# Every second tile of four residual additions moved from VectorE to GpSimd, in a two-model float32 kernel

## The reference, cut to what matters

```
x = x + _rms_norm(mix, norm_mix_post[layer])
hn = _rms_norm(x, norm_ffn_pre[layer])
x = x + _rms_norm(_squared_relu_mlp(hn, mlp_w1[layer], mlp_w2[layer]), norm_ffn_post[layer])
```

## Time and profile before

| | |
|---|---|
| median of 3 runs | 3810.01 us (3808.03 to 3811.25) |
| profiled execution, its own time | 3813.62 us |
| its span, first to last instruction | 3811.7 us |
| mean granted TensorE clock | 0.980 of full speed |
| busy: TensorE, VectorE, ScalarE, GpSimd | 95%, 49%, 31%, 8% of the span |

### The profile page before, as it was taken

One profiled execution on the slowest core, in us unless ns is written; L12 is line 12 of the kernel. 1 busy time (PEld: TensorE's weight loads), 2 busy tenths in 40 slices (PEclk: granted clock), 3 DMA queues, 4 the chain that ended last, 5 costly groups with the idle time before them and its releaser, 6 DMA issues.

```text
span 3811.7 us, 48355 instructions
## 1 busy us (share of the span) xinstructions
PE 3622.3 (95%) x17514; PEld 2500.3 (66%) x17514; DVE 1870.4 (49%) x3826; ACT 1173.1 (31%) x2184; POOL 307.6 (8%) x355
## 2 busy tenths in 40 slices
PE   5999999998889999979999999999898999999999
PEld 2445488883444888846666666666555788888874
DVE  3754463635554636434454454545403666666651
ACT  1202310102333101013444344434301455555540
POOL 6700000000000000000000000000000222222210
PEclk8999999999999999989999999999998999999999
DMA  7522333432013324231111011111011222222211
GB/s 155 143 78 61 98 102 89 111 81 60 24 50 89 100 78 122 78 93 30 34 33 33 28 33 33 33 33 31 25 50 47 62 61 61 61 61 61 61 47 61
DMA packets 456581, 246.46 MB, mean 65 GB/s; under 512 B 44272, under 2 KB 448496, under 8 KB 456464
## 3 DMA queue, kind: packets, MB, share of 16 engines
q1 hardware_dynamic: 420528, 216.28, 20.7%
q0 software_dynamic: 14144, 28.36, 2.8%
q10 hardware_dynamic: 21792, 0.22, 0.5%
HBM read 229.96 MB, written 14.80 MB: 64 GB/s over the span
## 4 chain that ended last, share of the span: by engine, by line
PE 88%; DVE 7%; issue 2%; ACT 2%; ACTq 1%; DMA 0%; DVEq 0%; SPq 0%
PE bank L487 19%; PE bank L1773 13%; PE bank L331 10%; PE bank L2325 9%; PE bank L1759 5%; PE bank L1057 3%; PE bank L2344 3%; PE bank L1230 3%; PE bank L1796 2%; PE bank L1127 2%; PE bank L884 2%; PE bank L1106 2%; PE bank L1741 2%; PE bank L867 1%; PE bank L1783 1%
## 5 line engine op out<-in xcount | busy, mean ns | idle before, releaser
L1773 PE MATMUL bank<-hT,ring 128*128 128x512 f32 x1504 | 510.3, 491 | 1.0 <-ACT arena L1976 1.0
L1773 PEld LDWEIGHTS bank<-hT,ring 128*128 128x128 f32 x1504 | 278.9, 190 | 218.4 <-issue 204.6
L331 PE MATMUL bank<-big,ring 128*128 128x512 f32 (+1 forms) x1024 | 394.0, 542 | 1.1 <-DVE big L2102 1.1
L331 PEld LDWEIGHTS bank<-big,ring 128*128 128x128 f32 x1024 | 192.5, 191 | 179.3 <-issue 171.0
L2375 POOL TENSOR_TENSOR tb<-ring 128x512 f32<-128x512 f32 x32 | 40.6, 1269 | 2898.2 <-DVE big L2850 2735.0
L1113 ACT ACTIVATE arena<-bank 128x512 f32<-128x512 f32 (+2 forms) x224 | 118.3, 528 | 448.3 <-PE bank L1106 447.5
L487 PE MATMUL bank<-big,arena 128*128 128x256 f32 x1024 | 228.9, 379 | 0.0
L487 PEld LDWEIGHTS bank<-big,arena 128*128 128x128 f32 x1024 | 194.7, 190 | 26.3
L2003 DVE TENSOR_REDUCE cols<-bank 128x1 f32<-128x768 f32 x128 | 116.5, 952 | 149.2 <-PE bank L1741 149.1
L1759 PEld LDWEIGHTS bank<-ring,hT 128*128 128x128 f32 x1536 | 175.2, 192 | 12.5 <-issue 12.5
L1759 PE MATMUL bank<-ring,hT 128*128 128x128 f32 x1536 | 178.3, 276 | 0.0
(11 more groups left out here) (338 smaller groups left out, 6056.3 us busy)
## 6 DMA issues: line engine op xcount, KB each, us to landing
ring<-in_mlp_w SPq DMA_DIRECT2D x128, 512.0 KB, 5.6
ring<-in_a_w_in SPq DMA_DIRECT2D x64, 512.0 KB, 4.0
ring<-in_b_w_in SPq DMA_DIRECT2D x64, 512.0 KB, 4.1
ring<-in_mod_w SPq DMA_DIRECT2D x48, 512.0 KB, 5.2
ring<-in_even_w_in SPq DMA_DIRECT2D x32, 512.0 KB, 3.9
bias_d<-tb POOLq DMA_DIRECT2D x96, 128.0 KB, 3.4
big<-bias_d POOLq DMA_DIRECT2D x16, 768.0 KB, 5.2
ring<-in_a_w_out SPq DMA_DIRECT2D x16, 512.0 KB, 4.0
```

Of the source, the lines that this page charges most:

```text
L331: mm = pe.matmul(bk(self.bank(n, j))[:, 0:z - a], ring[s][:, k % KT, :], self.rhs(k, a, z), start=k == order[0], stop=k == order[-1], skip ...
L1773: mm = pe.matmul(flatb[2][:, a:z], ring[s][:, k, :], hT[:, k, a:z], start=k == 0, stop=k == KT - 1)
```

## The change

In each of the four residuals the odd tiles are added to the stream by GpSimd, one addition per tile, as soon as VectorE's product of that tile is there. VectorE still multiplies all eight tiles, and adds the even ones: m0 m1 a0 m2 m3 a2 m4 m5 a4 m6 m7 a6. ScalarE waits for `r_x` before even tiles and for `kw_w` before odd ones. GpSimd's additions stand between its two old jobs. Nothing else in the program changes.

```diff
             for k in range(KT):
-                act.wait_ge(r_x, KT * r.i + k + 1)
+                if k % 2:
+                    act.wait_ge(kw_w, 1 + KT // 2 * r.i + k // 2 + 1)
+                else:
+                    act.wait_ge(r_x, KT // 2 * r.i + k // 2 + 1)
...
+        def pool_residual(pool, r):
+            for k in range(1, KT, 2):
+                pool.wait_ge(r_t, KT * r.i + k + 1)
+                pool.tensor_tensor(xT[:, k, 0:S], xT[:, k, 0:S], hT[:, k, 0:S], ALU.add).then_inc(kw_w, 1)
...
         def dve_residual(dve, r, g_post):
...
-                if k > 0:
+                if k % 2:
                     dve.wait_ge(r_t, KT * r.i + k)
                     dve.tensor_tensor(xT[:, k - 1, 0:S], xT[:, k - 1, 0:S], hT[:, k - 1, 0:S], ALU.add)\
                         .then_inc(r_x, 1)
...
         @block.gpsimd
         def _(pool):
             pool_bias(pool)
+            for r in res:
+                pool_residual(pool, r)
             pool_nat(pool)
```

## The result

The changed kernel takes 3819.27 us in the median of 15 runs (3817.55 to 3820.82), the kernel before 3811.31 in as many runs (3808.03 to 3816.79). The ratio is 1.0018, with a 95% interval of 1.0011 to 1.0025: 4 to 10 us slower, about 7 by the ratio and 8 by the medians. The profiled execution took 3819.81 us, 6.2 more than the one of before.

What follows compares the result with a forecast made beforehand. It took TensorE's products to bound nearly everything, with TensorE waiting in the residuals for the last tile; 3 x 1.35 + 1.5 = 5.6 us plus 0.9 for the clock gave +6.5, 3816.5 us, range 3806 to 3823.

Steps and rivals of the forecast that it cites:

- the four stretches: From each residual's first multiplication to the TensorE product it sets free: forecast to grow 5.6 us in all.
- the clock: TensorE, less busy in residuals 1 and 3, would run at a lower clock: 0.9 us in all, bounds 0 and 3.
- VectorE's paces: In the residuals, a multiplication starts 0.66 us and an addition 0.60 before the next instruction; four removed additions save 2.4.
- The turn and its price: GpSimd's additions alternate with VectorE's instructions in the residuals; each of the first three puts VectorE back 1.02 us.
- The signal from GpSimd to ScalarE: ScalarE hears of GpSimd's finished addition after 0.1 us, bounds 0.02 to 0.30.
- The last copy: ScalarE's last copy starts about 12.1 us after the first multiplication, not 10.79: +1.35 in residuals 0 to 2.
- step 5: Behind residuals 0 to 2 the delay moves on whole; in residual 3 TensorE's sum takes part of +1.8, leaving +1.5.
- the prediction's own sign: The prediction is wrong if the stretches from first multiplication don't grow, or if time went anywhere outside them.
- starvation: GpSimd's first addition in each residual starts only behind VectorE's last: +18 us in all, 3828 us; chance 0.13.
- the two don't shut each other out: GpSimd and VectorE run side by side in the residuals, ScalarE setting residuals 0 to 2: -3.5 us, 3806.5; chance 0.09.

Runs made afterwards that it cites:

- The PSUM version: The changed kernel with the reciprocal before each residual written to PSUM, so its multiplications read one SBUF input: 3804.73 us, ratio 0.998; again 3804.4 us, 0.9977.
- the signals alone: The kernel before with all additions still on VectorE, but counted on two semaphores that ScalarE waits for in turn: 3812.91 us, ratio 0.9999.

## Why the prediction was right

It gave 3816.5 us, +6.5; the medians of the same kernels differ by 8.0, the profiled executions by 6.2, and the ratio's interval is +4 to +10. The sign and the mechanism were right, and the time lies in the range; that it is less than 0.2% was given 0.59. That the sum came so close is partly luck: the four stretches were put 0.4 us too high, the clock 0.8 us too low and at the wrong place, and the two errors cancel in part (5.2 + 1.7 = 6.9 against 5.6 + 0.9 = 6.5). By its steps:

1. VectorE's paces, right: the two before an addition take 1.41 us and the next instruction starts 0.60 after an addition.
2. The turn and its price, right: GpSimd ends 1.13 us behind a0, and the pair behind it takes 2.42 for 1.41, 1.01 where 1.02 was forecast. What was only assumed, that a waiting GpSimd goes before the next multiplication, was shown by this profile and by the eight additions in strict alternation. The Trainium skill's rule ("SBUF — State Buffer", "Who interferes with whom"), that whoever issues first gets the shared port pair for the whole instruction, agrees with this trace. By the same section of the Trainium skill a VectorE instruction with at most one SBUF input, outside its two-port modes, does not contend with GpSimd. The PSUM version agrees: 743 ns.
3. The signal from GpSimd to ScalarE, oversized: in residual 0 the last copy starts at 457.13, and GpSimd's last addition (455.43, 1.65) ends at 457.08. It is 0.05 us where 0.1 was taken. The kernel with the signals alone shows that the second semaphore itself costs nothing.
4. The last copy at 12.02 for 12.1, so +1.23 and not +1.35 in residuals 0 to 2 (12.1 less 10.79 is 1.31, not the 1.35 that the step gave). With step 5, +1.46 for +1.5 in residual 3. The sum of the stretches is 5.2 for the 5.6 of the forecast.
5. That the delay passes whole: right in all four. In residual 2 TensorE's own sum still ended as before (its first product behind it comes 16.60 us after the first multiplication, before 16.62) and yet the stretch grew by 1.24, since the chain goes over VectorE's lines.
6. The term that was mis-sized and misplaced is TensorE's clock. The forecast put 0.9 us on residuals 1 and 3, where TensorE is on the chain. In both profiles of the changed kernel it is 1.7 us behind residual 0, in the products after VectorE's line 629. In residuals 1 and 3 nothing is left for the clock: residual 1 grew by 1.24, its last copy came 1.23 later, and residual 3 grew by 1.46, no more than the 1.5 that the forecast had without the clock. In residual 0 TensorE's own sum of squares was off the chain, as forecast; the clock that fell after line 629 was not looked for. By the prediction's own sign (it is wrong if the time went anywhere outside the stretches) these 1.7 us are a miss.

The rivals: starvation fell with the first profile, where GpSimd's additions stand between VectorE's, and with the eight additions. That the two don't shut each other out fell with the first profile; but its price, a gain of 3.5 us set by ScalarE's pace, is about what the four stretches gained (3.75) once the multiplications read PSUM.

## What to carry to other kernels

Before a VectorE instruction is moved to GpSimd, count the inputs in SBUF of what VectorE does beside it: if both read two, they run one after the other, here 1.68 us per tile where GpSimd alone takes 1.27. Put one input of VectorE's instructions into PSUM first where it fits there, and then the move is worth making: the same four additions that cost 1.23 to 1.46 us per residual then saved 0.53 to 1.60 against the kernel before. And look at the engine behind: with both free, ScalarE's 1.13 us per tile was the next bound in residuals 0 and 1, and TensorE's own sum in residual 2.

## What the runs showed of the hardware that was not expected

- With an instruction of either always ready, GpSimd and VectorE take turns one by one: eight multiplications and eight additions in 13.8 us, 1.68 per pair.
- TensorE's clock behind residual 0 was at its lower level (0.50, 1.2 GHz) for some 3 us in all three profiles where residual 0 was the changed one, and with two additions moved (2.50 and 3.11 us for the sixteen products that otherwise take 3.9 together); in none of the profiles of the kernel before, the signals alone, residuals 1 to 3 or the PSUM versions. With all eight additions moved, where the delay is largest, it was not low there (1.99) but behind residual 2 (3.78 and 3.02). Behind residual 0 TensorE had idled 2.27 or 2.28 us before these products every time, with the loss and without. So neither the length of the delay nor that of the idle time decides it alone; what does stays open.
- Reading one operand from PSUM instead of SBUF did not slow VectorE's multiplication (743 against 748 ns).
